# Gaps of 48 and 112 bytes between the activation chunks of two down projections

## The reference

```python
def swiglu(h, w_gate, w_up, w_down):
    return (jax.nn.silu(h @ w_gate) * (h @ w_up)) @ w_down
...
    u = jnp.einsum('bsd,df->bsf', h2, w_up[l])
    u = causal_depthwise_conv(u, w_conv[l], b_conv[l])
    u_val, u_gate = jnp.split(u, 2, axis=-1)
    y = jnp.einsum('bsf,fd->bsd', jax.nn.gelu(u_gate) * u_val, w_down[l])
```

## Time and profile before

| | us |
|---|---|
| Median of three runs | 982.19 |
| Lowest and highest of them | 981.73, 982.43 |
| Span of the profiled execution, first to last instruction | 980.3 |
| TensorE busy in it | 958.4 |
| VectorE, ScalarE busy in it | 720.6, 542.4 |
| Each of the three down projections (528 products) | 60.35 |

### The profile page before, as it was taken

The page is one execution under the profiler, slowest core; times in us unless marked ns, Lnnn a source line. Parts: engine busy times, 40 slices in busy tenths (PEclk is TensorE's granted clock), DMA queues, the critical chain, the costliest instruction groups (busy, mean ns, idle before and its releaser), DMA issues.

```text
span 980.3 us, 18888 instructions
## 1 busy us (share of the span) xinstructions
PE 958.4 (98%) x7971; PEld 923.9 (94%) x7971; DVE 720.6 (74%) x1340; ACT 542.4 (55%) x837; POOL 25.4 (3%) x54
## 2 busy tenths in 40 slices
PE   8999999999999999999999999999999999999997
PEld 8889999999998988899999997998999999999996
DVE  7965897777658777698879788555654879888653
ACT  7554664454447366565444545456755567666542
POOL 0300000000000000000000000000220000000000
PEclk9999999999999999999999999999999999999999
DMA  8536376766744734368767882653343545555621
GB/s 298 190 116 238 128 266 255 255 251 225 295 172 168 266 129 140 116 212 304 265 251 267 331 315 76 245 185 116 111 149 132 199 157 207 181 203 184 216 87 43
DMA packets 27588, 194.72 MB, mean 199 GB/s; under 512 B 3056, under 2 KB 3184, under 8 KB 4592
## 3 DMA queue, kind: packets, MB, share of 16 engines
q1 hardware_dynamic: 27504, 193.51, 54.7%
HBM read 192.45 MB, written 1.05 MB: 197 GB/s over the span
## 4 chain that ended last, share of the span: by engine, by line
PE 89%; ACT 4%; DVE 4%; issue 2%; DMA 1%; POOL 0%; SPq 0%; DVEq 0%; ACTq 0%
PE bank L508 25%; PE bank L509 24%; PE bank L514 23%; PE bank L639 2%; PE bank L665 2%; PE bank L569 2%; PE bank L563 2%; ACT s_whi L906 2%; PE bank L564 2%; PE bank L528 2%; PE bank L535 1%; PE bank L529 1%; PE bank L649 1%; DVE s_wlo L1382 1%; DMA s_xT<-in_xT 1%
## 5 line engine op out<-in xcount | busy, mean ns | idle before, releaser
L1382 DVE TENSOR_TENSOR s_wlo<-s_raw,s_whi 128x512 fp32r<-128x512 f32 (+1 forms) x364 | 372.3, 1065 | 138.1 <-ACT s_whi L906 137.9
L906 ACT ACTIVATE s_whi<-s_raw 128x1024 fp32r<-128x1024 f32 (+2 forms) x233 | 304.8, 1335 | 215.6 <-PE bank L514 205.9
L508 PE MATMUL bank<-s_hh,s_whi 128*128 128x256 f32 x1400 | 393.6, 281 | 1.1 <-DVE s_wlo L1382 0.7
L509 PE MATMUL bank<-s_hl,s_whi 128*128 128x256 f32 x1400 | 387.6, 277 | 0.0
L514 PE MATMUL bank<-s_hh,s_wlo 128*128 128x256 f32 x1383 | 382.8, 277 | 0.0
L508 PEld LDWEIGHTS bank<-s_hh,s_whi 128*128 128x128 f32 x1400 | 263.3, 188 | 6.9 <-issue 5.9
L509 PEld LDWEIGHTS bank<-s_hl,s_whi 128*128 128x128 f32 x1400 | 263.2, 188 | 0.1
L514 PEld LDWEIGHTS bank<-s_hh,s_wlo 128*128 128x128 f32 x1383 | 259.8, 188 | 0.0
L508 PE MATMUL bank<-s_ph,s_whi 128*128 128x256 f32 x528 | 146.4, 277 | 0.0
L509 PE MATMUL bank<-s_pl,s_whi 128*128 128x256 f32 x528 | 145.8, 276 | 0.0
L514 PE MATMUL bank<-s_ph,s_wlo 128*128 128x256 f32 x516 | 142.5, 276 | 0.0
(11 more groups left out here) (238 smaller groups left out, 1285.3 us busy)
## 6 DMA issues: line engine op xcount, KB each, us to landing
s_raw<-in_gu SPq DMA_DIRECT2D x44, 1024.0 KB, 4.9
s_raw<-in_dn SPq DMA_DIRECT2D x33, 1024.0 KB, 4.9
s_raw<-in_wada SPq DMA_DIRECT2D x24, 1024.0 KB, 5.7
s_raw<-in_up SPq DMA_DIRECT2D x22, 1024.0 KB, 4.9
s_raw<-in_wo SPq DMA_DIRECT2D x8, 1024.0 KB, 4.9
s_raw<-in_win_g SPq DMA_DIRECT2D x8, 1024.0 KB, 4.9
s_raw<-in_mla SPq DMA_DIRECT2D x4, 1024.0 KB, 5.4
s_raw<-in_wkv_v SPq DMA_DIRECT2D x4, 1024.0 KB, 4.9
```

What stands on the lines that cost most here:

```text
L508: e.matmul(out, hi, xh[:, k, :], start=first, stop=False, skip_group_check=True)
L509: e.matmul(out, hi, xl[:, k, :], start=False, stop=False, skip_group_check=True)
L906: e.activation(whi[w % SPLIT][:, at], raw[p % RAW][:, at], ACT.Copy).then_inc(S.hi.tick((w, c0)), 1)
L1382: e.tensor_tensor(wlo[s][:, at], raw[p % RAW][:, at], whi[s][:, at].bitcast(F32), ALU.subtract).then_inc(S.lo.tick((i, j), (i, "all")), 1)
```

## The change

`ph[layer]` and `pl[layer]` are allocated with more columns than they use and then cut back to 256. The chunks' pitch becomes 1,024 + 48 = 1,072 bytes in layer 0 and 1,024 + 112 = 1,136 bytes in layer 2; in layer 1 it stays 1,024. All else keeps its address.

```diff
+GAP = (12, 0, 28)
...
-                ph[layer] = sb(f"ph{layer}", [P, NF, T], F32R, scope)
-                pl[layer] = sb(f"pl{layer}", [P, NF, T], F32R, scope)
+                ph[layer] = sb(f"ph{layer}", [P, NF, T + GAP[layer]], F32R, scope)[:, :, 0:T]
+                pl[layer] = sb(f"pl{layer}", [P, NF, T + GAP[layer]], F32R, scope)[:, :, 0:T]
         with ExitStack() as scope:
-            shift(4 * 2 * NF * T, scope)
+            shift(4 * 2 * NF * (T + GAP[1]), scope)
             yg = sb("yg", [P, 8, T], F32, scope)
```

## The result

| | before | changed |
|---|---|---|
| Median of the runs | 982.31 (4 runs) | 989.41 (4 runs) |
| Lowest and highest | 981.73, 983.17 | 987.45, 990.38 |
| Span of the profiled execution | 980.3 | 986.9 |

The changed kernel takes 1.0066 times as long, with a 95% interval of 1.0053 to 1.0079. The medians differ by 7.1 us. The forecast was no change, 982.2 us, and the result lies above its range (979.3 to 985.9).

A forecast was written before the change was run, and what follows sets the result against it. The prediction took the start-to-start spacing of TensorE's products as the bound. All terms were 0: 980.3 + 0 + 0 + 0 + 0 = 980.3 us of span, with 1.9 us around it 982.2 us; range 979.3 to 985.9 us.

The forecast's parts named there:

- The work terms: Added and removed work in the gapped stages: no instruction comes or goes, ACT's and DVE's writes stay hidden; 0.
- The two rhythms: Spacing of the same product: 113.2 ns in a down projection, 117.8 ns in a gate and up stage.
- the quick rhythm itself: Term for 1,056 down-projection products at changed distances: taken as 0, between 4.9 us lost and 5.5 us gained.
- Plain float32 sums: Rows at L604 and L609, distances 128 and 416: 215 ns each, read as distance doing nothing there.
- The 512-column products: Value projection, L563: 114.4 ns per 256 columns with half the weight loads, read as the excess not coming from loads.
- the slow rhythm's 4.9 us: Upper bound on the cost in the gapped stages: 1,056 products x 4.6 ns if every one becomes slow.
- The choice of rhythm: Term for whether changed distances turn quick products slow in the gapped down projections: taken as 0, range 0 to 4.9 us.
- Distance alone doesn't choose the rhythm: Claim from down projection and gate and up stages: same distance modulo 512, yet 113.2 and 117.8 ns a product.
- Slow rhythm in the gapped stages: Rival: changing distances disturb the quick rhythm in gapped down projections; half slow 984.6 us, all 987.1 us; chance 0.20.
- The distance of before costs something: Rival: gapped down-projection products get quicker at better distances; half the excess gives 979.4 us, all 976.7 us; chance 0.15.
- the excess over 108 ns: Down-projection spacing of 113.2 ns against a 108 ns floor from float32 sums; 5.5 us if the gapped stages lost it.
- The stages behind turn over: Rival, after the first down projection: slow stretches cured, 979.9 us, chance 0.10; quick ones spoiled, about 984.5 us, chance 0.05.

## Why the prediction was wrong

**The frame was right.** TensorE's spacing bounds the down projections, and nothing else paid: the windows stayed free of waits, the middle stage stayed at 60.35 us. The work terms were 0 as put. The two rhythms of 113.2 and 117.8 ns are real, and a halved product does bring back the quick one.

**The step that failed is the term "the quick rhythm itself", the price of another distance, taken as 0.** It leaned on the wrong rows. Plain float32 sums at two distances were read as "distance does nothing". They take twice the time for each column and have no part in what the short form does. Both of their distances (128, and 416, which is 160 modulo 256) cost the short form 2.7 and 2.2 us a stage. The 512-column products compare shapes, not distances. The prediction named this doubt at its end, and it should have weighed more: no row had a short-form product at another distance, so the trace couldn't say that the distance is harmless. The term measured 4.90 us. Nor was the slow rhythm's 4.9 us a bound from above: at 196 modulo 256 two stages would lose 2 x 4.05 = 8.1 us.

**"The choice of rhythm", also taken as 0, came out right as a mechanism and for a weak reason.** No timing turned over: moved chunks were slow while they lasted, and the rounds behind them took 340 ns again. But that the rhythm survived for 22 chunks said nothing of gaps, since all these chunks stood at the same distance. The row showed that pieces and buffers may change, not that distances may. The 0 to 4.9 us that the prediction kept for this term were as large as the loss, and the range took in only three quarters of them.

**A sentence that was right for one distance was used for all.** "Distance alone doesn't choose the rhythm" came from two stages at the same distance. At 448 a stall chooses between 113.2 and 117.8 ns. At the 13 other places there is no choice: no round of three took less than 346 ns, where the quick rhythm takes 340.

**The rivals.** "Slow rhythm in the gapped stages" had the right size: 987.1 us if all products are slow, 4.9 us over before. That was luck. Its mechanism, a disturbance at each change of distance, is wrong: constant distances are as slow, and the products don't go over to the slow rhythm but take the price of their places, 3.7 to 7.7 ns each, which over the many places of the gapped stages came to a mean of 4.6. "The distance of before costs something" fell: none of 13 other places is better, and the excess over 108 ns stayed. "The stages behind turn over" does happen, but not by the change. The stretch at the start of the third block's gate and up stage was quick in the first run of the changed kernel and slow in the repeated one, worth 0.87 us, and it is quick in 6 of the 13 profiled executions, the one with all tiles moved together among them.

**The rule of the Trainium skill.** The page SBUF — State Buffer, section "Who interferes with whom", has an independent read port for each of TensorE's two operands and TensorE waiting on nobody, so that a distance would do nothing. The runs disagree: with the same instructions a down projection takes 60.35 us or 62.28 to 64.40 us by the distance between the two alone. The page TensorE: Matmul & The Clock Gate, section "Back-to-back issue gap", gives 109.2 ns for 256 columns, but for a product by itself, and says that in a stream with weight loads both set the spacing; the prediction left that condition out. The stream here never went below 113.2 ns.

**The remainder.** 7.1 us were measured and 4.9 explained. The profiled execution of the changed kernel lost 2.3 us before its first changed product, the repeated one nothing. The start varies with and without the change, and the prediction had no term for it.

**What stays open.** Why the one place is good, and why it returns after 256 bytes (of its 64 four-byte steps 14 were tried, so another good one isn't excluded); why good and bad products in turn cost more than their share; which weight tile is the partner, the one in use or the one being loaded, since all stand alike modulo 512; and why at the good place a stall can leave a second rhythm. At 64 modulo 256 every round beside the halved products takes 353 or 354 ns, the spacing of that slow rhythm; whether the two are one thing isn't known. What happens inside between the two streams was not seen, only its times.

## What to carry to other kernels

In a kernel like this one, bound by TensorE with a weight load for each short-form product, the distance between the moving operand and the weight tile is a tuning parameter: print it modulo 256 for every tile and keep it when tiles are added or resized, for an odd 64 bytes cost 26 us here. Before an effect is taken as zero, ask whether any row shows the same instruction with the parameter changed; if all rows have one value, the trace is silent and the range must reach to the end of the bound. Where like stages of a kernel take the same time to 0.01 us, their windows in one profile resolve what the medians of many runs can't.

## What the runs showed of the hardware

- A short-form (fp32r) product of 128x128 by 256 columns, with a weight load each, follows the one before after 113.2 ns if its chunk begins 192 bytes above a multiple of 256 from the weight tiles. At 13 other places it is 3.7 ns (240) to 7.7 ns (196) slower. The worst is 4 bytes from the best.
- It is the distance that counts: with all tiles moved by 64 bytes the stage takes 60.35 us, with the chunks alone or the weights alone moved to the same distance (128 modulo 256) 63.07 and 63.05 to 63.07 us.
- A single badly placed round (distance 0) costs 20 ns, 8 in its own 348 and 12 in the next one's 352, and the quick 340 ns are back behind that. In blocks the prices add up (half a stage at 0: 1.74 of 3.39 us). In turn with good ones they don't: every other chunk at 64 costs 1.83 of 2.27 us, and one product in three at 480 costs 2.82 us where all three cost 2.52.
- At the good distance a product in two halves brings back the quick rhythm that a stall had ended: with three of them more, 52 of 63 rounds of the `wbr` stage are quick, in 13 other executions at most 26.
- Pitches of 1,280 and 1,536 bytes between the chunks cost nothing (60.35 us).
- The granted clock fell to the 1.2 GHz level for 3.4 us between 13 and 19 us from the start in 8 of 15 profiled executions, whatever the edit: at 14.6 us in the first run of the changed kernel and not at all in the repeated one. In the 2.6 us ahead of it (12.0 to 14.6 us) TensorE was busy for 1.35 us in the one and 1.80 us in the other.
